# Cache copies of a hybrid decoder step, one 292-row piece per chunk of the projection in place of sixteen whole copies

## What is computed

```python
h = rmsnorm(x, norm_g)                                  # prompt: (2048, 1024)
proj = jnp.einsum('bld,de->ble', h, w_in)               # w_in: (1024, 4104)
...
k_ext = jnp.concatenate([k_win, kb], axis=1)            # k_win: (8, 2048, 8, 64), kb: (8, 4, 8, 64)
v_ext = jnp.concatenate([v_win, vb], axis=1)
...
new_k, new_v = k_ext[:, -2048:], v_ext[:, -2048:]       # outputs
```

## Time and profile before

| what | value |
|---|---|
| time, median of 3 runs | 2516.38 us (2516.11 to 2518.93) |
| span of the profiled execution, first to last instruction | 2518.4 us |
| PE busy | 2218.1 us, 88% of the span |
| PE weight load, DVE, ACT, POOL busy | 73%, 37%, 31%, 13% |
| data moved by DMA | 274.10 MB, of it 66.98 MB by POOL's queue |
| the 32 tiles of the projection | about 82 to 1025 us of the span |

### The profile page before, as it was taken

One profiled execution on the slowest core, in us unless ns is written; L12 is line 12 of the kernel. 1 busy time (PEld: TensorE's weight loads), 2 busy tenths in 40 slices (PEclk: granted clock), 3 DMA queues, 4 the chain that ended last, 5 costly groups with the idle time before them and its releaser, 6 DMA issues. The chain is left out here.

```text
span 2518.4 us, 40099 instructions
## 1 busy us (share of the span) xinstructions
PE 2218.1 (88%) x13254; PEld 1826.2 (73%) x13254; DVE 933.1 (37%) x2542; ACT 770.4 (31%) x1793; POOL 315.0 (13%) x332
## 2 busy tenths in 40 slices
PE   4787989899989989449998999899989986799997
PEld 3676878687868768139897989798979884466664
DVE  5440133114212411235454545455554544132221
ACT  5321122112112211124444444353534442222221
POOL 5200000000000000111111111111212114111110
PEclk9988999999999999769998999999999995899999
DMA  4526352735456373570404040404040104464641
GB/s 134 160 79 200 108 184 72 218 104 169 142 153 180 79 211 98 65 160 27 101 27 102 26 102 27 102 27 101 26 102 26 35 22 133 138 192 133 192 142 59
DMA packets 197558, 274.10 MB, mean 109 GB/s; under 512 B 37237, under 2 KB 159605, under 8 KB 188677
## 3 DMA queue, kind: packets, MB, share of 16 engines
q1 hardware_dynamic: 188852, 204.74, 30.9%
q0 software_dynamic: 1280, 66.98, 7.8%
q10 hardware_dynamic: 7248, 0.03, 0.2%
HBM read 201.70 MB, written 136.87 MB: 134 GB/s over the span
## 5 line engine op out<-in xcount | busy, mean ns | idle before, releaser
L265 PE MATMUL pj<-hT_hi,w_hi 128*128 128x512 f32 (+1 forms) x1056 | 427.9, 405 | 20.4 <-DVE w_lo L470 20.4
L266 PE MATMUL pj<-hT_lo,w_hi 128*128 128x512 f32 (+1 forms) x1056 | 417.0, 395 | 0.0
L267 PE MATMUL pj<-hT_hi,w_lo 128*128 128x512 f32 (+1 forms) x1056 | 416.0, 394 | 0.0
L1173 ACT ACTIVATE pt<-pt_ps 128x512 f32<-128x512 f32 (+2 forms) x320 | 170.9, 534 | 425.4 <-PE pt_ps L1116 425.2
L1124 PEld LDWEIGHTS o_ps<-vt,pt 128*128 128x128 f32 x2176 | 284.5, 194 | 18.6 <-issue 7.4
L1124 PE MATMUL o_ps<-vt,pt 128*128 128x64 f32 x2176 | 284.0, 271 | 0.0
L1251 DVE CUSTOM_DVE_ANT_0 sc<-s_ps,win 128x512 f32<-128x512 f32 (+2 forms) x320 | 193.0, 610 | 175.0 <-PE s_ps L1100 138.0
L265 PEld LDWEIGHTS pj<-hT_hi,w_hi 128*128 128x128 f32 (+1 forms) x1056 | 198.5, 188 | 67.7 <-DVE w_lo L470 18.2
L267 PEld LDWEIGHTS pj<-hT_hi,w_lo 128*128 128x128 f32 (+1 forms) x1056 | 198.1, 188 | 47.4 <-issue 0.6
L266 PEld LDWEIGHTS pj<-hT_lo,w_hi 128*128 128x128 f32 (+1 forms) x1056 | 198.7, 188 | 42.3 <-issue 0.6
L1167 ACT ACTIVATE sc<-sc,nmax 128x512 f32<-128x512 f32 (+2 forms) x320 | 207.9, 650 | 36.2 <-DVE nmax L1255 36.2
(11 more groups left out here) (358 smaller groups left out, 3190.5 us busy)
## 6 DMA issues: line engine op xcount, KB each, us to landing
out_dram<-in_cache_k_win_dram POOLq DMA_DIRECT2D x8, 4088.0 KB, 15.3
out_dram<-in_cache_v_win_dram POOLq DMA_DIRECT2D x8, 4088.0 KB, 27.7
w_raw<-in_w_in_dram SPq DMA_DIRECT2D x35, 512.0 KB, 9.6
qk_ch<-sil SPq DMA_DIRECT2D x32, 256.0 KB, 6.9
z_ch<-xr SPq DMA_DIRECT2D x32, 256.0 KB, 2.5
wqk<-hi SPq DMA_DIRECT2D x32, 256.0 KB, 3.2
wqk<-lo SPq DMA_DIRECT2D x32, 256.0 KB, 3.5
out_dram<-xr SPq DMA_DIRECT2D x32, 256.0 KB, 2.8
```

Source lines behind the costliest of these rows:

```text
L265: pe.matmul(out, w_hi[s][:, k, 0:m], hT_hi[:, k, cols], start=(k == 0), stop=False)
L266: pe.matmul(out, w_hi[s][:, k, 0:m], hT_lo[:, k, cols], start=False, stop=False)
L267: mm = pe.matmul(out, w_lo[s][:, k, 0:m], hT_hi[:, k, cols], start=False, stop=(k == KT - 1))
L1173: act.activation(pt[:, n % 4, 0:w], pt_ps[turned_bank((step, qb, *a[1:]))[0]][:, 0:w], ACT.Copy).then_inc(S["turned_out"], 1)
```

## The change

Each copy of 2044 rows is cut into seven of 292 rows (7 times 292 is 2044). A piece of K and a piece of V are issued in turn, each after one more chunk of the projection: the wait for `pj_done` goes by `16 * b + 2 * piece + y + 1`, so that of each 16 chunks the first 14 are followed by one piece. The count of the last wait and two constants follow.

```diff
+PIECES = 7
+PIECE = (PAST - DEC_SEQ) // PIECES
...
+            def shift(b, old, new, piece):
+                rows = slice(PIECE * piece, PIECE * piece + PIECE)
+                after = slice(PIECE * piece + DEC_SEQ, PIECE * piece + PIECE + DEC_SEQ)
+                pool.dma_start(new[bass.ds(b, 1), rows, :], old[bass.ds(b, 1), after, :]).then_inc(shifted, 16)
+
             with pool.Fori(0, DEC_BATCH) as b:
-                pool.wait_ge(pj_done, 16 * b + 1)
-                pool.sem_inc(seen, 1)
-                for old, new in ((D.cache_k, D.out_k), (D.cache_v, D.out_v)):
-                    pool.dma_start(new[bass.ds(b, 1), 0:PAST - DEC_SEQ, :], old[bass.ds(b, 1), DEC_SEQ:PAST, :]).then_inc(shifted, 16)
-            pool.wait_ge(shifted, 16 * 2 * DEC_BATCH)
+                for piece in range(PIECES):
+                    for y, (old, new) in enumerate(((D.cache_k, D.out_k), (D.cache_v, D.out_v))):
+                        pool.wait_ge(pj_done, 16 * b + 2 * piece + y + 1)
+                        pool.sem_inc(seen, 1)
+                        shift(b, old, new, piece)
+            pool.wait_ge(shifted, 16 * 2 * PIECES * DEC_BATCH)
```

## The result

The changed kernel takes 2427.2 us (median of four runs, 2425.82 to 2435.42) against 2517.65 (2516.11 to 2519.95): the ratio is 0.9649, with a 95% interval of 0.9633 to 0.9665. The forecast was 2427, in a range of 2418 to 2452.

What follows compares the result with a forecast made beforehand. PE bounds the kernel, idled or slowed by eight projection stalls behind the cache copies. From the profiled span, 2518.4 - 90.4 (stalls) + 1 (lost cover) = 2429.0 us; in terms of the runs' median 2427 us, range 2418 to 2452.

Steps and rivals of the forecast that it cites:

- The chain from DMA by ACT and DVE to PE: Projection: copies delay SP's loads and stores, ACT or DVE waits for these, and PE then idles; eight stalls.
- The 90.4 us from SP's intervals: Projection: total cost of eight stalls, from distances between SP's weight loads in disturbed and quiet tiles.
- The clean `k` to `v`: Interval between SP's weight loads without a stall, put at 28.62 us against 41.76 measured before; `wq` to `wk` likewise 24.31.
- The cost of a piece: DMA engines: each piece of a copy occupies each engine 1.75 to 2.0 us, at most 3.07.
- The load of the engines: DMA engines in the projection: pieces plus the quiet load keep them busy 0.50 to 0.73 of the time.
- The cover: Projection: stores have two chunks, about 12.6 us, before ACT is late; PE needs its `sam` only 10 us later.
- the rival of stalls that stay: Projection tiles: pieces still delay loads and stores, so some stalls remain; about 2452 us, up to 2472; chance 0.13.
- lost cover: First `hi` store of a tile behind pieces: up to 2 us in each of 8 tiles, 16 us; 1 taken.
- the few that I named as a sign: Profile after: no wait of ACT for `wqk` over a few us.
- the rival of a cost per chunk: Projection: each of 112 chunks pays for its piece; at 1.0 us each, 2538 us; chance 0.06.
- the block of 24.6 us: POOL's queue: two whole copies in a row, 8 pieces per engine at 3.07 us, hold back SP's transfers.
- The tail: Behind the projection loop: PE's 17.8 us wait for `w_lo` comes from a load issued behind the loop and stays.

Runs made afterwards that it cites:

- none: Kernel before with the cache copies left out altogether: 2426.34 us, ratio 0.9641 to the kernel before.
- burst: Changed kernel's 112 pieces, but all 14 of a sequence issued behind the one old wait: 2526.04 us, ratio 1.0032 to the kernel before.
- apart: Kernel before with its sixteen whole copies, but V issued eight chunks (two tiles) after K: 2428.68 us, ratio 0.9647.
- fine: Kernel before, old schedule, but copies issued as half rows to make small packets: 2452.44 us, ratio 0.9733.
- tail: Changed kernel, but SP waits for the last weight load to land before issuing the three small stores: 2423.87 us, ratio 0.9615 to the kernel before.

## Why the prediction was right

*The chain from DMA by ACT and DVE to PE* was right, and it was shown from both sides: without copies the time is the forecast's (none), and with the same pieces in a burst the stalls return (burst). That the median came out within 0.2 us of the forecast is luck beyond this: single runs of one kernel differ by up to 10 us, and the median before moved from 2516.38 to 2517.65 us with a fourth run.

*The 90.4 us from SP's intervals* hold: the loads, from first to last, take 90.1 us less (917.0 to 826.9). The clean `k` to `v` was put at 28.62 and is 28.65, the clean `wq` to `wk` at 24.31 and is 24.26. That the sum went beyond the waits that the profile lists, 72.0 us, by the matmuls at half clock was right too: where the sum left 18.4 us for them, PE's busy time fell by 24.4 us, 21.5 of it in the 32 tiles (855.8 to 834.3), and the granted clock is 0.99 from 95 to 931 us.

*The cost of a piece*, 1.75 to 2.0 us of each engine, came out at 2.0: 9.2% of 2433.9 us are 224 us, by 112. The load of the engines, 0.50 to 0.73, is 0.57. The estimate from the Trainium skill ("DMA: Bandwidth & Descriptors", anatomy of a DMA by the gpsimd path), 3.4 us per piece and 378 us in all, did not show as time of the DMA engines; it would be 15.5% of the span.

*The cover* was larger than I put it, and this is where the reading was too timid. I let a store land 12.6 us after its issue before ACT is late, and ACT be late by 10 us before PE is. In the kernel with whole copies apart DVE and ACT wait for stores up to 18.6 us, and its time is within 1.5 us of the changed kernel's. On the path over `sam` ACT may be late by 15.3 us, as the pairs of waits say: 17.3 on ACT and 2.0 on PE there, 24.0 and 8.7 in the kernel with small packets, 30.2 and 14.8 in the kernel before. With that, the rival of stalls that stay had less to stand on than the chance of 0.13 that I gave it. The 1 us that the sum allowed for lost cover did not appear (826.87 us against 826.82 without copies). The waits of ACT for `wqk` went up to 9.3 us, more than the few that I named as a sign, and cost PE nothing. Of the rival of a cost per chunk nothing showed; at twice the density 14 us were lost, in three places.

*What the forecast did not see* is that the cutting was not needed. I worked out the block of 24.6 us and called one piece per chunk the cure; two blocks of 12.3 us, two tiles apart, cure it as well.

*The tail* was left as it is, at about 18 us, and is, save in the profiled execution. There it cost 9.4 us more. Without that the span would be 2424.5 and not 2433.9, so 4.5 us below the 2429.0 that I summed; the spans of the other three runs, 2424.3 to 2426.2, are below it as well. The sum started from a span that was the longest of its four (its run took 2519.95 us, 2.3 over their median), and the 2.0 us that I took off for the median made up for most of it.

## What to carry to other kernels

A background transfer hurts by how long it holds back the packets of the others, not by its bytes or the number of its pieces. Here two things set that: how long its queue has work without a break (burst against the changed kernel, apart against before) and how large its packets are (fine). Two busy DMA queues passed packets in turn, so compare a turn of the big one with the number of packets that the small ones need, and the resulting delay with the cover (here 15.3 us on the path from a `wqk` store over ACT) of the engine that is the bound. When a stall's price is wanted, take the distances of a regular event in disturbed and quiet rounds; the listed waits leave out what the slower clock adds, a fifth of the whole here. Once the big blocks are gone, look for small ones of the same kind: three stores of 6 KB in tiny packets made PE wait 9.9 us when they were issued in the last `za` tile, and near the end of the mixers no such wait of PE shows.

## What the runs showed of the hardware

Two queues with packets of 57 KB and 0.5 KB on average pass them nearly one for one (128 to 112 in 22 us), and so do queues with 3.8 KB and 0.5 KB (902 to 896 in 18 us) and, in the burst of pieces, those from 222 to 234 us (199 to 199), though not before that (15 to 339 from 214 to 218 us). Half rows of 1 KB in a copy issued by POOL went out as packets of some 4 KB. The same 3584 packets of pieces occupied the engines for 7.2% of the span in a burst and 9.2% one by one: 1.6 and 2.0 us per piece. The last weight load of the projection, 512 KB in 512-byte packets, takes 11.1 us when the three stores of 4-byte packets are held back until it has landed (tail). With them issued right behind it, it takes 13.7 to 14.9 us in seven profiles, 11.2 in one (fine) and 23.6 in one (the first of the changed kernel).
